# GpSimd forms the last two result tiles itself and stores the first of them ahead of the last expert's rows

## The reference, cut to what matters

```
for e in range(N_EXPERTS):
    hid = jax.nn.silu(t @ w_expert_gate[e]) * (t @ w_expert_up[e])
    y = y + combine[:, e:e + 1] * (hid @ w_expert_down[e])
x = x + y
y_prompt, y_sample = rms_norm(xp, final_norm_g), rms_norm(xs, final_norm_g)
# rms_norm(x, g) = x * rsqrt(mean(x * x) + 1e-6) * g, row by row
```

## Time and profile before

| what | us |
|---|---|
| median of 3 runs (870.49 to 872.41) | 870.78 |
| the profiled execution's own time | 872.77 |
| its span (first to last instruction in the trace) | 870.6 |
| PE busy in it | 823.1 |
| POOL busy in it | 86.2 |

### The profile page before, as it was taken

The page is one execution under the profiler, slowest core; times in us unless marked ns, Lnnn a source line. Parts: engine busy times, 40 slices in busy tenths (PEclk is TensorE's granted clock), DMA queues, the critical chain, the costliest instruction groups (busy, mean ns, idle before and its releaser), DMA issues.

```text
span 870.6 us, 15977 instructions
## 1 busy us (share of the span) xinstructions
PE 823.1 (95%) x5347; PEld 749.2 (86%) x5347; DVE 602.8 (69%) x1030; ACT 517.3 (59%) x949; POOL 86.2 (10%) x75
## 2 busy tenths in 40 slices
PE   4999999999999999999999999999999999999990
PEld 3999999999999998988997887788888888888870
DVE  5373233787778777566446127799989999899974
ACT  7344214566666665555524232488888888888882
POOL 0000000000000000000000001122233222331121
PEclk9999999999999999999999999999999999999995
DMA  8622222133123311431335645799999999999975
GB/s 265 162 87 66 77 76 80 46 105 104 45 59 104 108 49 59 123 98 49 97 98 193 243 173 188 251 313 347 345 342 353 346 344 357 331 353 322 355 221 181
DMA packets 135959, 163.60 MB, mean 188 GB/s; under 512 B 18584, under 2 KB 103704, under 8 KB 135914
## 3 DMA queue, kind: packets, MB, share of 16 engines
q1 hardware_dynamic: 129818, 150.06, 51.9%
q0 software_dynamic: 5808, 12.36, 5.0%
q10 hardware_dynamic: 288, 0.59, 0.2%
HBM read 151.61 MB, written 20.12 MB: 197 GB/s over the span
## 4 chain that ended last, share of the span: by engine, by line
PE 87%; DMA 5%; DVE 3%; issue 3%; ACT 2%; POOL 0%; POOLq 0%; SPq 0%; ACTq 0%; DVEq 0%
PE ps L1601 25%; PE ps L1603 23%; PE ps L1602 23%; PE ps L1779 3%; PE ps L1795 2%; PE ps L1997 2%; PE ps L1742 1%; PE ps L1743 1%; PE ps L1788 1%; DMA sum_rows<-yb,ydn 1%; DMA fy<-sum_rows 1%; DMA gb<-in_norm_mix_g 1%; PE ps L2019 1%; PE ps L1919 1%; PE ps L1758 1%
## 5 line engine op out<-in xcount | busy, mean ns | idle before, releaser
L1498 DVE TENSOR_TENSOR wl<-rawM,wh 128x1024 fp32r<-128x1024 f32 x189 | 224.3, 1219 | 17.4 <-ACT wh L932 14.1
L932 ACT ACTIVATE wh<-rawM 128x1024 fp32r<-128x1024 f32 x192 | 195.5, 1055 | 9.5 <-PE ps L1603 3.9
L1601 PE MATMUL ps<-hTh,wh 128*128 128x272 f32 (+2 forms) x448 | 132.4, 296 | 2.5 <-DVE wl L1071 2.0
L1603 PE MATMUL ps<-hTh,wl 128*128 128x272 f32 (+2 forms) x448 | 130.8, 292 | 0.0
L1602 PE MATMUL ps<-hTl,wh 128*128 128x272 f32 (+2 forms) x448 | 130.1, 290 | 0.0
L1601 PE MATMUL ps<-wh,xh 128*128 128x256 f32 (+1 forms) x384 | 124.4, 324 | 0.0
L1603 PE MATMUL ps<-wh,xl 128*128 128x256 f32 (+1 forms) x384 | 121.8, 317 | 0.0
L1602 PE MATMUL ps<-wl,xh 128*128 128x256 f32 (+1 forms) x384 | 121.7, 317 | 0.0
L1601 PE MATMUL ps<-wh,hTh 128*128 128x384 f32 x256 | 93.9, 367 | 0.2 <-DVE mA L1180 0.2
L1601 PEld LDWEIGHTS ps<-hTh,wh 128*128 128x128 f32 x448 | 85.5, 191 | 4.7 <-issue 2.4
L1603 PE MATMUL ps<-wh,hTl 128*128 128x384 f32 x256 | 86.5, 338 | 0.0
(11 more groups left out here) (310 smaller groups left out, 1723.3 us busy)
## 6 DMA issues: line engine op xcount, KB each, us to landing
rawM<-in_w_expert_up SPq DMA_DIRECT2D x64, 512.0 KB, 10.9
rawM<-in_w_expert_down SPq DMA_DIRECT2D x64, 512.0 KB
rawM<-in_w_expert_gate SPq DMA_DIRECT2D x64, 512.0 KB
rawA<-in_w_in SPq DMA_DIRECT2D x64, 192.0 KB, 3.0
rawA<-in_w_in SPq DMA_DIRECT2D x20, 512.0 KB, 5.3
rawA<-in_w_attn_branch SPq DMA_DIRECT2D x8, 512.0 KB, 4.0
rawA<-in_w_out SPq DMA_DIRECT2D x8, 512.0 KB, 4.1
x<-in_x_prompt SPq DMA_DIRECT2D x4, 512.0 KB, 6.7
```

Source lines behind the costliest of these rows:

```text
L932: nc.scalar.activation(wh[:, (c + 1) % S, :], rawM[:, slot, :], ACT.Copy).then_inc(m_hi, 1)
L1498: V.tensor_tensor(wl[:, sl, :], rawM[:, slot, :], wh[:, sl, :].bitcast(F32), ALU.subtract).then_inc(m_lo, 1)
L1601: T.matmul(out, sh, mh_, start=start, stop=False, **kw)
L1603: return T.matmul(out, sl, mh_, start=False, stop=stop, **kw)
```

## The change

It concerns only what is done after the 15th item. On DVE, the two last calls of `final_rows` are gone: DVE still inverts the two roots (new `final_scale`), but earlier, between its steps on the last expert's rows, and no longer forms the rows. On POOL three new functions do the rest: `own_rows` multiplies `fy` by the gain into `ob`, `own_scale` multiplies that by the inverted root in place, and `own_store` issues the indirect store. Both multiplications are instructions of POOL itself. They stand after the gather of line 640 and ahead of the stores of the last expert's rows, and so does the store of tile 2; the store of tile 3 stays last.

```
+            def own_rows(j):
+                t = FINAL[j]
+                pool.wait_ge(fy_in[t], 16)
+                nc.gpsimd.tensor_tensor(ob[:, t, :], fy[:, t, :], gb[:], ALU.mult).then_inc(f_own, 1)
+
+            def own_scale(j):
+                t = FINAL[j]
+                pool.wait_ge(f_done, j + 1)
+                pool.wait_ge(f_own, j - 2)
+                nc.gpsimd.tensor_scalar(ob[:, t, :], ob[:, t, :], rsx[:, t:t + 1], None, ALU.mult).then_inc(f_own, 1)
+
+            def own_store(j):
+                t = FINAL[j]
+                pool.wait_ge(f_own, j)
+                pool.indirect_dma_start(o["y_prompt"][0], bass.IndirectOffsetOnAxis(ap=kept[:, ORDER.index(t):ORDER.index(t) + 1], axis=0),
+                                        ob[:, t, :], None, bounds_check=SEQ - 1, oob_is_err=False).then_inc(f_late, 16)
+            pool.wait_ge(m_lo, 24 * ip + 14)
+            pool.sem_inc(p_go, 1)
+            pool.wait_ge(gb_in, 48)
+            own_rows(3)
+            own_rows(4)
+            own_scale(3)
+            own_store(3)
+            own_scale(4)
             pool.wait_ge(ids_done, 1)
             pool.wait_ge(f_out, 16 * 3)
             pool.wait_ge(y15_done, 2)
...
-            for j in (3, 4):
-                t = FINAL[j]
-                pool.wait_ge(f_done, j + 1)
-                pool.indirect_dma_start(o["y_prompt"][0], bass.IndirectOffsetOnAxis(ap=kept[:, ORDER.index(t):ORDER.index(t) + 1], axis=0),
-                                        ob[:, t, :], None, bounds_check=SEQ - 1, oob_is_err=False).then_inc(f_late, 16)
+            own_store(4)
...
+                def final_scale(j):
+
+                    t = FINAL[j]
+                    dve.wait_ge(f_rt, j + 1)
+                    V.reciprocal(rsx[:, t:t + 1], rsx[:, t:t + 1]).then_inc(f_done, 1)
...
+                final_scale(3)
                 dve.wait_ge(y15_sum, 2)
                 link(V.tensor_tensor(xg[:, 1, :], yb[:, 1, :], gb[:], ALU.mult))
+                final_scale(4)
...
-                for j in range(3, NT):
-                    final_rows(j)
```

More of the change, by code:

```diff
@@ L308, in build @@
         f_out, f_rt, f_done = (sem(n) for n in ("f_out", "f_root", "f_done"))
-        ids_done, f_late = sem("ids_done"), sem("f_late")
+        ids_done, f_late, f_own = sem("ids_done"), sem("f_late"), sem("f_own")
         acc_in, wgt_done, lw_mm, lw_done = sem("acc_in"), sem("wgt_done"), sem("lw_mm"), sem("lw_done")
```

## The result

The changed kernel takes 876.47 us (median of 6 runs, 875.58 to 878.05) against 871.39 us for the kernel before (6 runs, 870.49 to 872.44): a ratio of 1.0059 with a 95% interval of 1.0047 to 1.0071, which is 5.1 us slower, between 4.1 and 6.2. The prediction said 871.2 us and no measurable change; the time lies above the range that it gave.

What follows compares the result with a forecast made beforehand. POOL's last store, behind tile 3's landing, bounds the end; five terms start the last expert's rows at 862.98, 1.72 later, less 1.28 for one store: +0.44 on 870.78 gives 871.2 us, range 869.9 to 874.0.

Steps and rivals of the forecast that it cites:

- The string: Serial work at the kernel's end, from tile 3's sums landing (856.27) to POOL's last store: 865.31 before, 865.75 forecast.
- DVE's freed time: DVE's two products, 2.6 us, moved to POOL: worth nothing, since they ended 2 us before they were needed.
- its cover: POOL's product of tile 2: sums there by 852.84, so even 2.9 us of work ends before tile 3 lands at 856.27.
- terms 2 and 4 of the sum: POOL's scalings of tiles 2 and 3: 1.1 us each, one pass and 0.18; 0.92 to 2.0 for tile 2.
- My own sign of being wrong: The prediction is wrong if a single POOL product takes over 3 us, or the end hangs on something else.
- 1 product of tile 3: POOL's product of tile 3, starting at about 856.32: 2.0 us, between 0.92 and 2.93.
- 3 store of tile 2, with its gap: POOL's store of tile 2, waiting for the scaling's semaphore: 0.86 + 1.0 us.
- 5 gap: POOL's gap before the last expert's rows: 0.6 us, between 0.30 and 0.86.
- start; two stores that follow: Start of POOL's product of tile 3 at about 856.32; steps of 1.42 + 1.35 us behind the last expert's rows.
- Rival B: At the end, POOL and DVE block each other when reading SBUF: 0.7 to 1.2 us more, 871.9 to 872.4; chance 0.27.
- DVE's slip: DVE's steps held by POOL's first product: the last expert's rows about 1.3 us late, hidden behind POOL.
- Rival C: POOL's products and scalings at the end are slow, at their high ends: +3.5 us, 874.3 us; chance 0.15.

Runs made afterwards that it cites:

- e1: The kernel before, with POOL's store of tile 2 ahead of the last expert's rows, DVE still forming both tiles: ratio 0.9981 to the kernel before.
- e9: The same kernel as e1, timed again: ratio 0.9987 to the kernel before.
- e10: As e1, but DVE forms tile 2 one place earlier, right behind tile 1: ratio 0.9988 to the kernel before.
- e5: The kernel before, with nine POOL instructions timed one by one behind its last store: scaling 2.85 us, copy 1.04; total time not compared.
- e12: The kernel before, with pairs of POOL and DVE instructions started together behind its last store: POOL's copy 2.02 us for 1.04; total time not compared.
- e11: The changed kernel, with POOL's two scalings replaced by copies of the tile onto itself: ratio 1.0018 to the kernel before, 1.6 us.

## Why the prediction was wrong

**What held.** The string, its start and its end did: the time moved with the start of POOL's last store (4.8 us in the traces, 5.1 in the times), the store that leaves the string is worth 1.3 us (e1, e9, e10), DVE's freed time is worth nothing (e1, e9 and e10 leave both products with DVE and still gain), a store behind POOL's own result starts 0.86 us after it (0.86 measured). The first product had its cover and ended at 855.2, before tile 3 landed.

**The step that failed: terms 2 and 4 of the sum, the scalings.** I took 1.1 us each, with 2.0 as the high end, because the only large row of POOL was a clearing, and I let an instruction cost as many passes as it has large inputs. Alone the scaling takes 2.85 (e5), above the end of my range and above the product of two tensors that I had priced at 2.0. The counting came out for a copy, 1.04 against my 1.1, and not for the scaling. My own sign of being wrong, a single product over 3 us, did appear (3.82). Term by term, measured less mine:

| term | mine | measured | difference |
|---|---|---|---|
| 1 product of tile 3 | 2.0 | 2.35 | +0.35 |
| 2 scaling of tile 2 | 1.1 | 3.82 | +2.72 |
| 3 store of tile 2, with its gap | 1.86 | 2.00 | +0.14 |
| 4 scaling of tile 3 | 1.1 | 2.86 | +1.76 |
| 5 gap | 0.6 | 0.17 | -0.43 |
| start; two stores that follow | | | -0.03; -0.18 |

This adds to +4.3, and with the +0.44 of the prediction to the 4.8 of the trace. Of the +2.72, 1.75 are the scaling's own price and 0.97 its wait for DVE's product with the gain.

**Rival B came true as a mechanism, and was a part only.** DVE and POOL do block each other, if not always for the whole of an instruction (e12). The price of 0.7 to 1.2 us on POOL's string was right (0.97; 1.0 in e11), and DVE's slip made the last expert's rows 0.94 us late (I had said about 1.3), hidden behind POOL as said. I gave it 0.27 for want of any row of POOL reading SBUF.

**Rival C was the nearest in sign, and wrong in size and cause.** It made all products slow, 3.5 us in all. The product was close to my value (2.35 for 2.0; the estimate of 2.25 from the Trainium skill, GPSIMD Engine Reference, section 3.1 Elementwise, was nearer still), the scalings beyond C's bound of 2.0. With the scalings at 1.1 the kernel is 1.6 us slower by its ratio (e11), inside my range; so the range failed by this one price.

**What stays open.** Why this form takes 2.85 us for 1024 columns where a product with a repeated number takes 1.89 was not looked into; the runs show only that neither the number per row, nor working in place, nor other engines' work is the cause.

## What to carry to other kernels

An engine's instruction is priced by a row of its own form: a scaling on GpSimd costs 2.85 us for 128x1024, a copy 1.04 and a product of two tensors 2.35, and no counting of tensors read and written would have told so. Where the trace has no such row and the sum turns on it, the upper bound must be several times the nearest row, or the form must be measured alone first. And when the aim is to reorder a queue, try the reordering alone: here it was worth its 1.3 us without any work moved to the slower engine.

## What was not expected of the hardware

On GpSimd, multiplying a 128x1024 tile by one number per row took 2.85 us as a scaling and 1.89 us as a product with that number repeated along the row, and even the scaling by a constant took 2.77. The Trainium skill (GPSIMD Engine Reference, section 4.1 Engine selection) says of GpSimd that instructions with one input run roughly at line rate: the copy agrees with 1.04 us, the scaling does not.
